# Four plain tiles instead of six, a pass of the output projection of their own, and a last pass that adds to a sum put into PSUM

## The chip, the cores and the metric

The kernel runs on one core of a Trainium2 chip. The metric is the device time of one execution in microseconds; lower is better. The inputs are already in the chip's memory when the time begins.

## The reference, cut to what matters

Two request groups (512 prompt tokens and 32 sample tokens, 544 in all) go through two layers of a streaming encoder. Each layer is feed-forward, mixer, feed-forward, so there are four feed-forward blocks; they take most of the time, and the change is in them alone.

```python
def swiglu(x, w_gate, w_up, w_down):
    a = jnp.einsum('btd,df->btf', x, w_gate)      # d = 1024, f = 2816
    b = jnp.einsum('btd,df->btf', x, w_up)
    return jnp.einsum('btf,fd->btd', jax.nn.silu(a) * b, w_down)
# in each layer, with gains g of the norms:
x = x + 0.5 * rms_norm(swiglu(rms_norm(x, g[0]), ...), g[1])
x = x + rms_norm(mixer(rms_norm(x, g[2])), g[3])
x = x + 0.5 * rms_norm(swiglu(rms_norm(x, g[4]), ...), g[5])
```

## The kernel before

**Numbers in two parts.** All matrix products are float32-accurate, made of three passes of the engine's rounded float32: each factor is split into a high part (ScalarE, a copy that rounds) and a low part (VectorE, the factor minus its high part), and `mm3` issues high x high, high x low and low x high. So each product of a 128x128 weight tile with 272 tokens is three matmuls, and the tokens come in two halves, H = 0 and 1. One weight set is loaded by SyncE's queue into `w_raw` (four slots of 128x1024, two groups of two units in flight), split into `w_hi` and `w_lo`, and used by TensorE. A slot's next load waits until its low part is made; its next high part waits until TensorE has left it.

**A feed-forward block** has 22 hidden tiles of 128 and runs in this order on TensorE:

1. The plain part: hidden tiles 0 to 5, one after the other. `in_half` makes gate and up of one tile for one half: 2 x 8 x 3 = 48 matmuls, so 96 a tile and 576 in all. VectorE takes each result out of PSUM times the norm's factor, ScalarE applies silu, and the two split the hidden tile.
2. The other 16 hidden tiles are eight pairs. For a pair, gate (step q even) and up (q odd) are 2x2 block products made with seven block products instead of eight: `seven`, 7 x 4 x 3 = 84 matmuls a step. Its left factors (parts of x and their sums, `part_of`) are made during the plain part; its right factors are sums of weight blocks (`sums`, three instructions on VectorE), split in four pieces (`split_seven`).
3. The output projection ("down") comes in two parts, because not all hidden tiles fit at once. Part 0 covers hidden tiles 0 to 9 (six plain, two pairs) and stands behind the first four steps of `seven`; part 1 covers tiles 10 to 21 behind the other twelve. A part is 16 units (m, H): output tile m of 8, half H. `down_unit` runs a unit in two pieces, u = 0 for the first eight hidden tiles and u = 1 for the rest; the first four units run all their u = 0 pieces ahead of their u = 1 pieces. Part 0's results are copied from PSUM to `y` by ScalarE (`down_half`); part 1's are added to `y` by VectorE (`add_half`), and ScalarE then squares and scales them (`down_result`).

The loops that call these on PE, ACT and DVE are written out by hand, and so is each engine's order; nothing is reordered later. GpSimd sums the squares. At a block's end (`boundary`, `update` on the engines) VectorE adds the normed result to x half by half, and the next sub-layer's first `in_half` waits tile by tile for `xlo`.

**Lines.** `mm3` is L777 to L779. L631 and L634 are the high and the low part of a plain or output weight, L676 and L679 those of a product step, L657 to L661 the sums, L1684 and L2042 the split of the left factors, L1989 the read of a gate, L2005 the low part of a plain hidden tile, L2068 that of a pair, L1625 `down_half`, L1635 the square, L1921 `add_half`, L1976 `xlo`.

## Time and profile before

| | |
|---|---|
| time, median of 3 runs | 1950.31 us (1947.32 to 1950.62) |
| the profiled execution | 1950.23 us; its span 1948.3 us |
| TensorE busy | 1927.8 us, 15984 matmuls |
| VectorE busy | 1274.9 us |
| ScalarE busy | 1012.5 us |
| GpSimd busy | 204.5 us |
| granted TensorE clock | 0.997 of full |

The span runs from the first to the last instruction of the execution; the time holds 1.9 us around it. A busy time is the sum over an engine's instructions. Matmuls overlap, each of them is recorded with some 0.29 us, so how fast they follow one another is read from windows (time over count) and not from the duration of one.

### The profile page before, as it was taken

The numbers are of one execution on the slowest core, as the hardware profiler recorded it, in microseconds if no ns is written. First come the engines' busy times: TensorE is split into PE (matmuls) and PEld (weight loads), VectorE is DVE, ScalarE is ACT, GpSimd is POOL, SyncE is SP. The second block draws the span as 40 slices with busy tenths as digits, with TensorE's granted clock in tenths as the row PEclk, the third lists the DMA queues.
The fourth block names the chain that finished last, engine by engine and source line by source line (L and its number), as shares of the span: only waits on it lengthen the run. The fifth ranks groups of instructions, "written<-read, shape, count | busy, mean of one in ns | idle before, by whom it ended". The sixth has DMA issues, their size and how long they took to land.

```text
span 1948.3 us, 38106 instructions
## 1 busy us (share of the span) xinstructions
PE 1927.8 (99%) x15984; PEld 1875.3 (96%) x15984; DVE 1274.9 (65%) x1652; ACT 1012.5 (52%) x1925; POOL 204.5 (10%) x221
## 2 busy tenths in 40 slices
PE   9999999999999999999999999999999999999997
PEld 9999999999669999999999999999997999999997
DVE  7853884674673886378559844784667488448845
ACT  7443664531584655366546543664438555436642
POOL 0000000200362100000020000001236200000012
PEclk9999999999999999999999999999999999999999
DMA  5232323332311222233323123222341221232232
GB/s 181 73 95 93 109 87 98 98 104 77 122 45 44 78 75 88 87 109 108 94 82 108 66 82 112 90 103 86 107 123 47 75 93 66 82 114 87 103 91 70
DMA packets 59018, 177.90 MB, mean 91 GB/s; under 512 B 7057, under 2 KB 15585, under 8 KB 58721
## 3 DMA queue, kind: packets, MB, share of 16 engines
q1 hardware_dynamic: 56720, 167.66, 26.5%
q0 software_dynamic: 2128, 7.80, 1.3%
q8 instruction: 128, 2.10, 0.5%
q14 instruction: 42, 0.34, 0.1%
HBM read 168.26 MB, written 5.36 MB: 89 GB/s over the span
## 4 chain that ended last, share of the span: by engine, by line
PE 93%; DVE 5%; issue 1%; ACT 1%; DMA 0%; DVEq 0%; SPq 0%; ACTq 0%
PE psum L779 29%; PE psum L777 29%; PE psum L778 28%; PE psum L1091 1%; PE psum L1077 1%; PE psum L1210 1%; DVE y L1894 1%; DVE xlo L1976 1%; PE psum L999 1%; DVE rstd L1883 1%; DVE w_lo L634 1%; PE psum L1054 1%; PE psum L1193 1%; PE psum L1165 1%; DVE x L1901 1%
## 5 line engine op out<-in xcount | busy, mean ns | idle before, releaser
L777 PE MATMUL psum<-xhi,w_hi 128*128 128x272 f32 x1824 | 529.8, 290 | 1.7 <-DVE xlo L1976 1.3
L779 PE MATMUL psum<-xhi,w_lo 128*128 128x272 f32 x1824 | 525.7, 288 | 0.0
L778 PE MATMUL psum<-xlo,w_hi 128*128 128x272 f32 x1824 | 524.9, 288 | 0.0
L779 PE MATMUL psum<-h_hi,w_lo 128*128 128x272 f32 x1216 | 351.6, 289 | 0.0
L777 PE MATMUL psum<-h_hi,w_hi 128*128 128x272 f32 x1216 | 349.8, 288 | 0.0
L778 PE MATMUL psum<-h_lo,w_hi 128*128 128x272 f32 x1216 | 349.6, 287 | 0.0
L777 PEld LDWEIGHTS psum<-xhi,w_hi 128*128 128x128 f32 x1824 | 343.5, 188 | 5.7 <-DVE xlo L1976 2.3
L634 DVE TENSOR_TENSOR w_lo<-w_raw,w_hi 128x1024 fp32r<-128x1024 f32 (+1 forms) x198 | 204.2, 1058 | 214.6 <-ACT w_hi L631 214.5
L778 PEld LDWEIGHTS psum<-xlo,w_hi 128*128 128x128 f32 x1824 | 343.4, 188 | 0.4
L779 PEld LDWEIGHTS psum<-xhi,w_lo 128*128 128x128 f32 x1824 | 342.8, 188 | 0.0
L631 ACT ACTIVATE w_hi<-w_raw 128x1024 fp32r<-128x1024 f32 (+1 forms) x198 | 170.2, 882 | 203.9 <-PE psum L779 203.8
L679 DVE TENSOR_TENSOR w_lo<-w_raw,w_hi 128x1024 fp32r<-128x1024 f32 x128 | 156.5, 1223 | 117.5 <-ACT w_hi L676 116.1
L778 PEld LDWEIGHTS psum<-h_lo,w_hi 128*128 128x128 f32 x1216 | 229.0, 188 | 0.0
L777 PEld LDWEIGHTS psum<-h_hi,w_hi 128*128 128x128 f32 x1216 | 228.8, 188 | 0.0
L779 PEld LDWEIGHTS psum<-h_hi,w_lo 128*128 128x128 f32 x1216 | 228.5, 188 | 0.0
L777 PE MATMUL psum<-corner,w_hi 128*128 128x272 f32 x768 | 221.8, 289 | 2.1 <-DVE w_lo L679 2.1
L778 PE MATMUL psum<-corner,w_hi 128*128 128x272 f32 x768 | 222.1, 289 | 0.0
L779 PE MATMUL psum<-corner,w_lo 128*128 128x272 f32 x768 | 222.1, 289 | 0.0
L676 ACT ACTIVATE w_hi<-w_raw 128x1024 fp32r<-128x1024 f32 x128 | 135.1, 1055 | 37.3 <-PE psum L779 37.3
L779 PE MATMUL psum<-xlo,w_lo 128*128 128x272 f32 x512 | 148.2, 290 | 0.0
L777 PEld LDWEIGHTS psum<-corner,w_hi 128*128 128x128 f32 x768 | 144.8, 189 | 3.1 <-DVE w_lo L679 2.9
L778 PE MATMUL psum<-xhi,w_hi 128*128 128x272 f32 x512 | 147.4, 288 | 0.0
(301 smaller groups left out, 3556.3 us busy)
## 6 DMA issues: line engine op xcount, KB each, us to landing
w_raw<-in_w_gate_up SPq DMA_DIRECT2D x172, 512.0 KB, 4.1
w_raw<-in_w_down SPq DMA_DIRECT2D x64, 512.0 KB, 3.6
w_raw<-in_w_down SPq DMA_DIRECT2D x32, 256.0 KB, 3.7
w_raw<-in_even_in SPq DMA_DIRECT2D x16, 512.0 KB, 3.9
w_raw<-in_odd_in SPq DMA_DIRECT2D x10, 512.0 KB, 4.3
w_raw<-in_w_down SPq DMA_DIRECT2D x32, 128.0 KB, 3.6
w_raw<-in_even_out SPq DMA_DIRECT2D x8, 512.0 KB, 3.8
w_raw<-in_odd_out SPq DMA_DIRECT2D x8, 512.0 KB, 4.3
```

The lines of the kernel that those rows point to most:

```text
L631: nc.scalar.activation(hi[:, cols], raw, ACT.Copy).then_inc(w_hi_done, 1)
L634: nc.vector.tensor_tensor(lo[:, cols], raw, hi[:, cols].bitcast(F32), ALU.subtract).then_inc(w_lo_done, 1)
L676: nc.scalar.activation(hi, raw, ACT.Copy).then_inc(w_hi_done, 1)
L679: nc.vector.tensor_tensor(lo, raw, hi.bitcast(F32), ALU.subtract).then_inc(w_lo_done, 1)
L777: nc.tensor.matmul(out, s_hi, m_hi, start=first, stop=False, skip_group_check=skip)
L778: nc.tensor.matmul(out, s_hi, m_lo, start=False, stop=False, skip_group_check=skip)
L779: return nc.tensor.matmul(out, s_lo, m_hi, start=False, stop=last, skip_group_check=skip)
L999: return nc.tensor.matmul(psum[rows, b, cols], q, k, start=False, stop=True, skip_group_check=True)
L1054: nc.tensor.matmul(psum[rows, bank + e, c:c + w], qN[r, p, q:q + 64], kN[r, p, 0:w], start=i < 2, stop=True, skip_group_check=True)
L1077: mm = nc.tensor.transpose(psum[0:kw, 4 + e, j * P:(j + 1) * P], pr[:, e, col:col + kw], ident[:])
L1091: return nc.tensor.matmul(psum[64 * e:64 * e + 64, bank, cols], v, probs, start=first, stop=True, skip_group_check=True)
L1165: mm = nc.tensor.matmul(psum[64 * half:64 * half + 64, bank + d, cols], qtC[r, tile, q0:q0 + HD], kdup[r, tile // 4, keys], start=True, st ...
```

## The change

The plain part shrinks to four hidden tiles, and nine pairs take the other 18 (18 steps, six of them ahead of part 0). The plain tiles get a pass of the output projection of their own, `first_pass`, right behind them: 16 units over four hidden tiles each, whose weights are four new groups ("first", 512 columns a unit). ScalarE copies its results into tiles 4 to 7 of `h_gate` and `h_raw` (`hold`). Part 0 then covers the six hidden tiles of the first three pairs (four in u = 0, two in u = 1); VectorE adds its results to the held ones and writes `y` (`add_held`). Part 1 covers twelve hidden tiles as before, but its PSUM banks are filled first with `y` by ScalarE (`put`), its matmuls add to what is there (no `start`), and ScalarE squares and scales straight out of PSUM; `add_half` is gone. `unit_tiles`, the loads and the waits for freed slots follow the new sizes.

```diff
-PLAIN = 6
-KDOWN = (10, 12)
+PLAIN = 4
+KDOWN = (6, 12)
+UNIT = (4, 8)
+HIDDEN = ((0, 1, 2, 3, 8, 9), tuple(range(12)))
+HELD = 4
 PAIRS = [(f, f + 1) for f in range(PLAIN, KF, 2)]
 SEVEN = 2 * len(PAIRS)
-SEVEN_A = KDOWN[0] - PLAIN
+SEVEN_A = KDOWN[0]
...
-KINDS = {"ffn": [("in", f) for f in range(PLAIN)] + [("seven", q) for q in range(SEVEN_A)] +
+KINDS = {"ffn": [("in", f) for f in range(PLAIN)] + [("first", i) for i in range(4)] + [("seven", q) for q in range(SEVEN_A)] +
...
         def pair_tiles(p):
-            f = PAIRS[p][0]
-            t = f if f < KDOWN[0] else f - KDOWN[0]
+            t = HIDDEN[0][2 * p] if 2 * p < KDOWN[0] else HIDDEN[1][2 * p - KDOWN[0]]
             return slice(t, t + 2)
+        def held(m, H):
+            return (h_gate if m < KD // 2 else h_raw)[:, HELD + m % 4, HALF[H]]
...
-                    pe.wait_ge(y_added, 2 * KD * (ffn_no(s) - 1) + 14)
+                    pe.wait_ge(y_scaled, 2 * KD * (ffn_no(s) - 1) + 14)
...
-                        pe.wait_ge(proj_read, P0[s] + 2 * PLAIN - 4 + (2 if name == "T1" else 1) + q)
+                        pe.wait_ge(first_read, 2 * KD * n + 9 + banks[name])
...
-                    hidden = KDOWN[0] * part + (KDOWN[part] if u else KD)
-                    pe.wait_ge(hlo_ready, 2 * PLAIN * (n + 1))
-                    pe.wait_ge(pair_lo, len(PAIRS) * n + (hidden - PLAIN) // 2)
+                    hidden = KDOWN[0] * part + (KDOWN[part] if u else UNIT[part])
+                    pe.wait_ge(pair_lo, len(PAIRS) * n + hidden // 2)
                 bank = DOWN_BANKS[part][down_order(part).index((m, H)) % 4]
-                for k in range(KD, last + 1) if u else range(KD):
-                    w = slice((k - KD * u) * P, (k - KD * u + 1) * P)
-                    mm = mm3(psum[:, bank, 0:TH], hi[:, w], lo[:, w], h_hi[:, k, HALF[H]], h_lo[:, k, HALF[H]],
-                             k == 0, k == last)
+                for k in range(UNIT[part], last + 1) if u else range(UNIT[part]):
+                    w, t = slice((k - UNIT[part] * u) * P, (k - UNIT[part] * u + 1) * P), HIDDEN[part][k]
+                    mm = mm3(psum[:, bank, 0:TH], hi[:, w], lo[:, w], h_hi[:, t, HALF[H]], h_lo[:, t, HALF[H]],
+                             k == 0 and part == 0, k == last, part > 0)
...
+            def first_pass(s):
+                n = ffn_no(s)
+                def some(i, tiles):
+                    m, H, bank = i // 2, i % 2, i % 8
+                    g, u = G0[s] + PLAIN + m // 2, m % 2
+                    pe.wait_ge(w_lo_done, splits_at(g) + u + 1)
+                    for k in tiles:
+                        w = slice(k * P, (k + 1) * P)
+                        mm = mm3(psum[:, bank, 0:TH], w_hi[:, slot(g, u), w], w_lo[:, slot(g, u), w],
+                                 h_hi[:, k, HALF[H]], h_lo[:, k, HALF[H]], k == 0, k == PLAIN - 1)
+                    return mm
+                pe.wait_ge(hlo_ready, 2 * (PLAIN * (n + 1) - 1))
+                for i in range(6):
+                    if i in (0, 4):
+                        pe.wait_ge(proj_read, P0[s] + 2 * PLAIN - (0 if i else 2))
+                    some(i, range(PLAIN - 1))
+                pe.wait_ge(hlo_ready, 2 * PLAIN * (n + 1))
+                for i in range(6):
+                    some(i, (PLAIN - 1,)).then_inc(first_done, 1)
+                for i in range(6, 2 * KD):
+                    if i >= 8:
+                        pe.wait_ge(first_read, 2 * KD * n + i - 7)
+                    some(i, range(PLAIN)).then_inc(first_done, 1)
             def down(s, part):
...
+                                pe.wait_ge(first_read, 2 * KD * (n + 1))
...
                         elif u == 0:
-                            if i == 0:
-                                pe.wait_ge(corner_added, 2 * (SEVEN * (n + 1) - 1))
-                                pe.wait_ge(corner_copied, 2 * (SEVEN * (n + 1) - 1))
-                            elif i == 3:
-                                pe.wait_ge(corner_added, 2 * SEVEN * (n + 1))
-                                pe.wait_ge(corner_copied, 2 * SEVEN * (n + 1))
+                            pe.wait_ge(y_put, 2 * KD * n + i + 1)
...
-                    pe.wait_ge(y_added if part else y_half, 2 * KD * n + i - 3)
+                    pe.wait_ge(*((y_put, 2 * KD * n + i + 1) if part else (y_half, 2 * KD * n + i - 3)))
...
+            def hold(s, i):
+                act.wait_ge(first_done, 2 * KD * ffn_no(s) + i + 1)
+                nc.scalar.activation(held(i // 2, i % 2), psum[:, i % 8, 0:TH], ACT.Copy).then_inc(first_read, 1)
             def down_result(s, i):
                 order = down_order(1)
                 m, H = order[i]
-                act.wait_ge(y_added, 2 * KD * ffn_no(s) + i + 1)
+                whole = psum[:, DOWN_BANKS[1][i % 4], 0:TH]
+                act.wait_ge(y_ready, y_event(s, m, H) + 1)
                 if i >= 4:
                     act.wait_ge(ysq_summed, total_event(s, *order[i - 4]) + 1)
-                nc.scalar.activation(scratch[:, i % 4, :], y[:, m, HALF[H]], ACT.Square).then_inc(ysq_ready, 1)
-                nc.scalar.activation(y[:, m, HALF[H]], y[:, m, HALF[H]], ACT.Copy,
+                nc.scalar.activation(scratch[:, i % 4, :], whole, ACT.Square).then_inc(ysq_ready, 1)
+                nc.scalar.activation(y[:, m, HALF[H]], whole, ACT.Copy,
                                      scale=post_gains[:, s, m:m + 1]).then_inc(y_scaled, 1)
+                if 4 <= i + 3 < 2 * KD:
+                    put(s, i + 3)
+            def put(s, i):
+                n, (m, H) = ffn_no(s), down_order(1)[i]
+                if i == 0:
+                    act.wait_ge(y_half, 2 * KD * (n + 1))
+                    act.wait_ge(corner_added, 2 * (SEVEN * (n + 1) - 1))
+                elif i == 3:
+                    act.wait_ge(corner_added, 2 * SEVEN * (n + 1))
+                elif i >= 4:
+                    act.wait_ge(y_scaled, 2 * KD * n + i - 3)
+                nc.scalar.activation(psum[:, DOWN_BANKS[1][i % 4], 0:TH], y[:, m, HALF[H]], ACT.Copy).then_inc(y_put, 1)
...
                         part_high(s, 3)
+                for i in range(2 * KD):
+                    hold(s, i)
+                    if i == 1:
+                        split_unit(act, "act", g + PLAIN + 2, 0)
+                    elif i == 3:
+                        split_unit(act, "act", g + PLAIN + 2, 1)
                         part_high(s, 4)
+                    elif i == 5:
+                        split_unit(act, "act", g + PLAIN + 3, 0)
+                    elif i == 7:
+                        split_unit(act, "act", g + PLAIN + 3, 1)
+                        part_high(s, 5)
+                        part_high(s, 6)
+                    elif i in (9, 11, 13, 15):
+                        split_seven(act, "act", s, 0, (i - 9) // 2)
+                keep(s, 0, "B11")
...
+                                for i in range(3):
+                                    put(s, i)
                             split_unit(act, "act", down_group(s, part, 0), 1)
...
-                        for i in range(2 * KD):
-                            down_half(s, i)
-                            if i == 1:
-                                split_unit(act, "act", down_group(s, 0, 2), 1)
-                            elif i in (2, 5, 6, 9, 10):
-                                split_group(act, "act", down_group(s, 0, {2: 3, 5: 4, 6: 5, 9: 6, 10: 7}[i]))
-                            elif i in (13, 14):
-                                split_seven(act, "act", s, SEVEN_A, i - 13)
+                        split_unit(act, "act", down_group(s, 0, 2), 1)
+                        for m in range(3, KD):
+                            split_group(act, "act", down_group(s, 0, m))
+                        split_seven(act, "act", s, SEVEN_A, 0)
...
                     load_table(ACT.Sqrt)
+                    put(s, 3)
...
+            def add_held(s, i):
+                n, (m, H) = ffn_no(s), down_order(0)[i]
                 if i == 0:
-                    dve.wait_ge(y_half, 2 * KD * (n + 1))
-                dve.wait_ge(y_ready, y_event(s, m, H) + 1)
-                half = y[:, m, HALF[H]]
-                nc.vector.tensor_tensor(half, half, psum[:, DOWN_BANKS[1][i % 4], 0:TH], ALU.add).then_inc(y_added, 1)
+                    dve.wait_ge(first_read, 2 * KD * (n + 1))
+                dve.wait_ge(y_ready, y_event(s, m, H, 0) + 1)
+                nc.vector.tensor_tensor(y[:, m, HALF[H]], held(m, H), psum[:, DOWN_BANKS[0][i % 4], 0:TH],
+                                        ALU.add).then_inc(y_half, 1)
...
+                        split_unit(dve, "dve", down_group(s, 0, 2), 0)
+                        for i in range(2 * KD):
+                            add_held(s, i)
+                            if i == 2:
+                                split_unit(dve, "dve", down_group(s, 0, 2), 1)
+                            elif i in (3, 6, 7, 10, 11):
+                                split_group(dve, "dve", down_group(s, 0, {3: 3, 6: 4, 7: 5, 10: 6, 11: 7}[i]))
+                            elif i == 13:
+                                sums(dve, s, SEVEN_A)
+                            elif i == 14:
+                                split_seven(dve, "dve", s, SEVEN_A, 0)
+                                split_seven(dve, "dve", s, SEVEN_A, 1)
                         continue
                     split_unit(dve, "dve", down_group(s, 1, 2), 0)
...
-                        add_half(s, i)
```

Three places on two engines, as the built programs have them; numbers in brackets are the semaphores that an instruction waits for.

The first is ScalarE behind the split of the third left factor (`part_high`, `corner_56`). Before, the last two plain tiles follow (L1601 silu, L1606 high part of h), mixed with the splits for the first product step (L676):

```order
L1601 ACTIVATE gate_even<-gate_even 128x544 [waits gate_scaled]
L1606 ACTIVATE h_hi<-gate_even 128x544 [waits h_ready]
L676 ACTIVATE w_hi<-w_raw 128x1024 [waits proj_ready,raw_in0]
L676 ACTIVATE w_hi<-w_sum 128x1024 [waits proj_ready,w_summed]
L1684 ACTIVATE xhi<-sum_63 128x4x272 [waits proj_ready,part_ready]
L1684 ACTIVATE xlo<-sum_66 128x4x272 [waits proj_ready,part_ready]
L676 ACTIVATE w_hi<-w_raw 128x1024 [waits proj_ready,w_summed]
L1601 ACTIVATE scratch<-scratch 128x544 [waits gate_scaled]
```

After, the 16 copies of `hold` (L1663) stand there, with the splits of the first pass's last two groups (L645) and of the product step (L690) between them:

```order
L1737 ACTIVATE xhi<-sum_63 128x4x272 [waits proj_ready,part_ready]
L1663 ACTIVATE h_gate<-psum 128x272 [waits first_done] x2
L645 ACTIVATE w_hi<-w_raw 128x512 [waits first_done,raw_in0]
L1663 ACTIVATE h_gate<-psum 128x272 [waits first_done] x2
L645 ACTIVATE w_hi<-w_raw 128x512 [waits first_done,raw_in1]
L1737 ACTIVATE xlo<-sum_66 128x4x272 [waits proj_ready,part_ready]
L1663 ACTIVATE h_gate<-psum 128x272 [waits first_done] x2
```

The silu and high-part steps of two plain tiles went, sixteen reads of PSUM came, and the product step's splits moved behind the ninth of them.

The second is VectorE where output part 0 ends and the next product step's weights are made. Before, the low parts of output tile 7 (L634), the sums (L657 to L661) and the product step's low parts (L679) follow one another without a wait for a result:

```order
L634 TENSOR_TENSOR w_lo<-w_raw,w_hi 128x1024 [waits w_hi_done]
L634 TENSOR_TENSOR w_lo<-w_raw,w_hi 128x256 [waits w_hi_done]
L657 TENSOR_TENSOR w_sum<-w_raw 128x1024 [waits w_lo_done,raw_in1,raw_in0]
L659 TENSOR_TENSOR w_raw<-w_raw,w_sum 128x512 [waits w_summed]
L661 TENSOR_TENSOR w_sum<-w_raw 128x512 [waits w_summed]
L679 TENSOR_TENSOR w_lo<-w_raw,w_hi 128x1024 [waits w_hi_done]
L679 TENSOR_TENSOR w_lo<-w_sum,w_hi 128x1024 [waits w_hi_done]
```

After (`add_held` is L1976, the low parts L648 and L693, the sums L671 to L675):

```order
L648 TENSOR_TENSOR w_lo<-w_raw,w_hi 128x512 [waits w_hi_done]
L648 TENSOR_TENSOR w_lo<-w_raw,w_hi 128x256 [waits w_hi_done]
L1976 TENSOR_TENSOR y<-h_raw,psum 128x272 [waits y_ready] x2
L671 TENSOR_TENSOR w_sum<-w_raw 128x1024 [waits w_lo_done,raw_in1,raw_in0]
L673 TENSOR_TENSOR w_raw<-w_raw,w_sum 128x512 [waits w_summed]
L675 TENSOR_TENSOR w_sum<-w_raw 128x512 [waits w_summed]
L1976 TENSOR_TENSOR y<-h_raw,psum 128x272 [waits y_ready]
L693 TENSOR_TENSOR w_lo<-w_raw,w_hi 128x1024 [waits w_hi_done]
L693 TENSOR_TENSOR w_lo<-w_sum,w_hi 128x1024 [waits w_hi_done]
L1976 TENSOR_TENSOR y<-h_raw,psum 128x272 [waits y_ready]
```

The adds of units 12 to 15 (four, the first two in one row), which wait for TensorE, now stand between them.

The third is VectorE at the boundary behind part 1 of the first block. Before, `add_half` (L1921) stands between the steps of `update` (L1894 and L1901) and of `xlo` (L1976):

```order
L1894 TENSOR_TENSOR y<-y,rstd 128x2x272
L1901 TENSOR_TENSOR x<-x,y 128x2x272 [waits dve_step]
L1976 SCALAR_TENSOR_TENSOR xlo<-x,gains,xhi 128x272 [waits xhi_ready] x2
L1921 TENSOR_TENSOR y<-y,psum 128x272 [waits y_ready]
L634 TENSOR_TENSOR w_lo<-w_raw,w_hi 128x1024 [waits w_hi_done] x2
L1901 TENSOR_TENSOR x<-x,y 128x2x272 [waits dve_step]
```

After, the same steps (L1952, L1959, L2030) with no add between them:

```order
L1952 TENSOR_TENSOR y<-y,rstd 128x2x272
L1959 TENSOR_TENSOR x<-x,y 128x2x272 [waits dve_step]
L2030 SCALAR_TENSOR_TENSOR xlo<-x,gains,xhi 128x272 [waits xhi_ready] x2
L648 TENSOR_TENSOR w_lo<-w_raw,w_hi 128x1024 [waits w_hi_done] x2
L1959 TENSOR_TENSOR x<-x,y 128x2x272 [waits dve_step]
```

The add went; two more went from the same stretch, one between two earlier steps of `update` and one behind the `xlo` rows that follow, and one from ahead of it.

## Rows read from the trace of the kernel before

**Rows 1.** The page: engines' busy time, and the clock granted to TensorE in 40 slices.

```profile
PE 1927.8 (99%) x15984; PEld 1875.3 (96%) x15984; DVE 1274.9 (65%) x1652; ACT 1012.5 (52%) x1925; POOL 204.5 (10%) x221
...
PEclk9999999999999999999999999999999999999999
```

**Rows 2.** The page: the chain that ended last, by engine.

```profile
PE 93%; DVE 5%; issue 1%; ACT 1%; DMA 0%; DVEq 0%; SPq 0%; ACTq 0%
```

**Rows 3.** Windows, TensorE alone: busy (instructions), clock, DMA share, GB/s.

```profile
124.00:184.20 60.20, 60.20 (x481) 1.00 0.31 100
184.20:310.80 126.60, 126.60 (x1009) 1.00 0.28 97
310.80:383.50 72.70, 72.70 (x581) 1.00 0.32 96
```

**Rows 4.** Whom TensorE waited for: us in total, times, longest us.

```profile
PE psum L777 <- DVE w_lo L679: 2.1, 4, 0.5
...
PE psum L777 <- DVE xlo L1976: 1.3, 4, 0.6
```

**Rows 5.** Timeline of TensorE where the second product step begins: start, us.

```profile
91.21 0.29 PE L779 MATMUL psum<-xlo,w_lo 128*128 128x272 f32 x1
92.01 0.39 PE L777 MATMUL psum<-corner,w_hi 128*128 128x272 f32 x1 [0.52 <-DVE w_lo L679]
```

**Rows 6.** The same at the boundary behind the first feed-forward block.

```profile
386.14 0.29 PE L779 MATMUL psum<-xhi,w_lo 128*128 128x272 f32 x1
386.54 0.39 PE L777 MATMUL psum<-xhi,w_hi 128*128 128x272 f32 x1
...
398.82 0.28 PE L779 MATMUL psum<-xhi,w_lo 128*128 128x272 f32 x1
399.28 0.39 PE L777 MATMUL psum<-xhi,w_hi 128*128 128x272 f32 x1 [0.18 <-DVE xlo L1976]
```

**Rows 7.** Timeline of VectorE at that boundary.

```profile
380.25 0.42 DVE L1921 TENSOR_TENSOR y<-y,psum 128x272 f32<-128x272 f32 x1
```

**Rows 8.** Timeline of the end of the kernel, VectorE and ScalarE.

```profile
1936.18 0.44 DVE L1921 TENSOR_TENSOR y<-y,psum 128x272 f32<-128x272 f32 x1 [3.44 <-PE psum L779]
1936.65 0.43 ACT L1635 ACTIVATE scratch<-y 128x272 f32<-128x272 f32 x1 [3.67 <-DVE y L1921]
```

**Rows 9.** Timeline of VectorE behind plain tile 3, and at the first product steps.

```profile
56.82 0.72 DVE L1989 TENSOR_TENSOR scratch<-psum,rstd 128x544 f32<-128x544 f32 x1 [2.00 <-PE psum L779]
...
60.99 0.72 DVE L2005 TENSOR_TENSOR h_lo<-scratch,h_hi 128x544 fp32r<-128x544 f32 x1
...
88.16 1.22 DVE L657 TENSOR_TENSOR w_sum<-w_raw 128x1024 f32<-128x1024 f32 x1
...
90.74 1.22 DVE L679 TENSOR_TENSOR w_lo<-w_raw,w_hi 128x1024 fp32r<-128x1024 f32 x1
```

**Rows 10.** Timeline of VectorE behind the first product stage.

```profile
128.18 1.29 DVE L2068 TENSOR_TENSOR h_lo<-h_raw,h_hi 128x1088 fp32r<-128x1088 f32 x1 [0.85 <-ACT h_hi L1676]
```

**Rows 11.** VectorE ahead of the second product stage, and the loads it needs (SPq).

```profile
172.35 1.23 DVE L657 TENSOR_TENSOR w_sum<-w_raw 128x1024 f32<-128x1024 f32 x1 [1.19 <-DMA w_raw<-in_w_gate_up]
...
167.10 4.56 SPq L706 DMA_DIRECT2D w_raw<-in_w_gate_up  x4
```

**Rows 12.** Groups on VectorE by shape: busy, mean ns | idle before.

```profile
L679 DVE TENSOR_TENSOR w_lo<-w_sum,w_hi 128x512 fp32r<-128x512 f32 x64 | 43.8, 684 | 0.0
...
L1921 DVE TENSOR_TENSOR y<-y,psum 128x272 f32<-128x272 f32 x64 | 27.9, 436 | 119.7 <-PE psum L779 119.3
```

**Rows 13.** Groups on ScalarE by shape.

```profile
L631 ACT ACTIVATE w_hi<-w_raw 128x1024 fp32r<-128x1024 f32 x135 | 140.3, 1054 | 177.2 <-PE psum L779 177.2
...
L676 ACT ACTIVATE w_hi<-w_sum 128x512 fp32r<-128x512 f32 x64 | 40.5, 632 | 23.6 <-PE psum L779 23.6
...
L1625 ACT ACTIVATE y<-psum 128x272 f32<-128x272 f32 x64 | 25.0, 390 | 92.3 <-PE psum L779 92.3
...
L1684 ACT ACTIVATE xhi<-sum 128x1088 fp32r<-128x1088 f32 x8 | 8.8, 1105 | 0.0
```

104 lines of the change are left out of this document (39 added, 65 removed).

## The prediction

> **What bounds the kernel now.** First the page's busy times and clock row, then the chain that ended last, then windows of TensorE alone. The first shows TensorE busy for 1927.8 of 1948.3 us at full clock, VectorE for two thirds and ScalarE for half [rows 1]; the second puts 93% of the chain on TensorE [rows 2]. So time goes only where matmuls are removed or where TensorE stands still. The windows give its pace: output part 0 (480 matmuls and one neighbour) takes 60.20 us, the last twelve product steps (1008) 126.60 us, output part 1 with its neighbours 72.70 us [rows 3]: 60.20/480 = 0.1254 and 126.60/1008 = 0.1256 us a matmul, the same in the product steps and in the projection. No window holds a hole. So 0.1256 us is what one matmul is worth.
>
> Then the holes. The table of waits names two kinds, four times each [rows 4]. One is where the second product step of a block begins: starts 0.80 us apart where the pace is 0.13, so 0.67 us lost, waiting for the low part of a weight [rows 5]; all four blocks have it. VectorE began the sums for that step at 88.16 and ended the first low part at 90.74 + 1.22 = 91.96 [rows 9]; it was late because the last plain tiles, the left factors' low parts and the first step's weights had all been queued ahead. The other is behind a block: starts 0.40 and 0.46 us apart, so 0.27 + 0.33 = 0.60 us lost [rows 6]; three blocks have a feed-forward or mixer stage behind them. Last, behind the final unit, VectorE's add (0.44 us) and then ScalarE's square stand on the chain with nothing beside them [rows 8].
>
> **The change, part by part.** *Matmuls.* Two plain tiles cost 2 x 96 = 192, the pair that replaces them two steps of 84 = 168. The projection stays at 22 x 8 x 2 x 3 = 1056 a block, in three passes. So 24 fewer a block, 96 in all: 96 x 0.1256 = **-12.1 us**. TensorE's load of weights is in the pace already.
>
> The Trainium skill's page "TensorE: Matmul & The Clock Gate", section "Back-to-back issue gap", gives a gap of columns/2.4 + 2.5 ns at full clock, for 272 columns 116 ns, and says that pairs of weight load and matmul are paced by both. By its formula the term would be 11.1 us; the row's 125.6 ns decides.
>
> *The new pass at its start.* E is the end of the last plain `in_half`. The six first units take hidden tiles 0 to 2 (54 matmuls, 6.8 us) before tile 3 is wanted. Behind plain tile 3 today, VectorE starts at 56.82 and its low part ends at 61.71, 4.9 us later [rows 9]; it will be shorter by half of two splits. Slack 1.9 us. The four plain tiles no longer have a fifth behind them, and this is what hides them instead.
>
> *Its second weight pair.* Unit 8 starts at E + 96 x 0.1256 = 12.1 us and wants the low part of group 2, which VectorE makes behind the tile's low part (4.9), two sums of left factors and three low parts of them (five of 1.29) and then 0.68 [rows 9, 10, 12]: 12.0 us by full durations. But consecutive instructions start some 0.08 us sooner than that, and the two splits ahead take 0.68 and not 1.22. So about 11 us, no wait; from the other side, 0.3 us a block.
>
> *VectorE up to the product steps.* By the same durations, everything between E and the last piece of the first step is 25.1 us: 4.9 - 1.1 for tile 3, nine instructions of 1.29 for the left factors (the row of their shape), 4 x 0.68 for splits, the sums 2.58 (88.16 to 90.74), 3 x 1.22 + 0.68 for the pieces [rows 9, 10, 12]; besides it waits for the splits' high parts (ScalarE's last comes behind its copy of unit 15, near E + 25). TensorE wants the first piece at E + 24.1 and the last 9 us after. The first is ready three pieces earlier, near 22. No wait; and the sums of the second step now start at E + 26 for a step at E + 34.7, where before they ran late. So the first kind of hole closes: 4 x 0.67 = **-2.7 us**.
>
> *ScalarE in the pass.* 16 copies of 0.39, four splits of 0.63, three left factors of 1.11, 3 x 1.05 + 0.63 for the step's pieces [rows 13]: 15.9 of 24.1 us. PSUM has eight banks, so a unit may come seven later than its copy. Free.
>
> *Six steps and not four ahead of part 0.* The same steps as the twelve of the window, which have no hole. Free beyond their matmuls.
>
> *Part 0.* Its first pieces now cover only 4 x 12 x 0.1256 = 6.0 us and not 12.1, and then the last pair is wanted. Today its low part ends at 128.18 + 1.29 = 129.47, 5.5 us behind the part's start at 124.0 [rows 3, 10]. ScalarE and VectorE each split 512 and not 1024 columns ahead of it, so nearer 4.7. Slack 0.6 to 1.3 us. A unit now lasts 18 x 0.1256 = 2.26 us and not 3.77. Its u = 0 weights go into a slot that TensorE leaves 0.75 us ahead of the end of a unit and are wanted 2.26 us behind that end: 3.0 us for a high part (0.63), the add that waits for the unit's end (0.44) and the low part (0.68) [rows 12, 13], 0.75 + 0.44 + 0.68 = 1.9 us. Slack 1.1 us. The adds are on VectorE, which idled there.
>
> *Part 0 to the next product step.* With S the start of that step, unit 13 ends at S - 4.5. VectorE adds (0.44), sums (2.58), adds (0.44) and makes the first low part (1.22) [rows 9, 12], which comes to S + 0.2 by full durations and S by overlapped ones, plus some 0.1 for the signals. Today all this lies far ahead: the sums began at 172.35, 11.9 us before 184.20 [rows 3, 11]. The loads take 172.35 - 167.10 = 5.3 us [rows 11]; issued behind tile 6's low part, which follows the add of unit 10 (end S - 11.3, + 0.44 + 0.68 = S - 10.2), they land at S - 4.9, before the sums want them. So 0 to 0.5 us a block, I take 0.2: **+0.8 us**.
>
> *Puts.* ScalarE writes three banks inside the last product step (3 x 0.39) and the fourth behind the last pair; TensorE wants that one 9 us into part 1. The trace has no copy from `y` to PSUM; the nearest row is the copy the other way, 0.39 [rows 13], and a block's sixteen would be 6.2 us of ScalarE's idle half. Each later put comes two units (9 us) ahead of its unit. Free; if not free at the part's start, 0.4 a block.
>
> *Boundary.* Three adds of 0.43 [rows 7] leave VectorE's queue ahead of the `xlo` that TensorE waits for, two before the first hole and all three before the second; ScalarE's square comes an add earlier. Both holes (0.27, 0.33) are shorter than that. ScalarE's put there fills an idle stretch. 3 x 0.60 = **-1.8 us**. At the very end the add goes: 1936.65 - 1936.18 = **-0.5 us** [rows 8].
>
> *Loads.* The same bytes in more pieces; queued behind the same kind of wait. Nothing.
>
> Sum: -12.1 - 2.7 + 0.8 - 1.8 - 0.5 = -16.3 us. Against the profiled execution's 1950.23 us that is 1933.9; the median of the runs, 1950.31, is 0.1 above it. **I predict 1934 us.** 0.2% (4 us) is what a measurement of this kernel tells from no change.
>
> **Rivals.** *(1) The holes stay or move, only the matmuls go.* VectorE gets 16 adds into its densest stretches, and three slacks above are about a microsecond. If the closed holes come back as others of their size and part 0's end costs its upper bound, 0.5: 1950.2 - 12.1 + 2 = 1940; with the second weight pair and the puts at their bounds too, (0.3 + 0.4) x 4 = 2.8, 1943. For it: the slacks; against it: each is positive by rows. 1937 to 1943.
>
> *(2) PSUM is emptied too slowly.* Three passes are read out instead of two, 16 reads more and 16 writes more a block, all by ScalarE. It decides when ScalarE's work in the first pass passes 24.1 us; it is 15.9, so each of those copies would have to take 0.9 and not 0.39 us. Then TensorE waits 0.5 us or more a unit, and at 0.5 us on 16 units in four blocks, +32 us, 1966. The Trainium skill, page "Trainium Kernel Development and Optimization", section "Best Practices", says to mind PSUM pressure, as a denser TensorE does not speed up its evacuation; the rows have ScalarE half idle.
>
> *(3) Slower by part 0's short units.* If high part, add and low part for a unit's weights take longer than 3.0 us, each of twelve units waits. The gain is used up at 16.3/48 = 0.34 us each, so when the 1.9 us become 3.35; at 0.5 us, +24 - 16 = +8, 1958. It would need a load that lands late or an add that waits a full unit. No row shows either.
>
> *(4) Nothing moves,* because another engine already paces TensorE: 1950. Against it, a pace equal to 0.2% in two stages with different partners.
>
> **How the numbers follow.** My forecast (1930.5 to 1937): 0.66. Rival 1: 0.22. Rivals 2 and 3: 0.04 each. Rival 4: 0.02; what I have not thought of: 0.02, either side. The range takes the forecast and most of rival 1: 1930 to 1941. Faster by over 0.2% (below 1946.4): 0.90; within: 0.04; slower: 0.06.
>
> **What would show it.** TensorE with 96 matmuls fewer in its count; windows of product steps and of part 0 still at 0.1256 us a matmul; no wait for a low part at a block's second product step; starts at the boundaries 0.13 us apart; a new small wait for a low part where part 0 ends; the square on the chain right behind the last matmul. The prediction is wrong if part 0's window is longer than 288 x 0.1256 = 36.2 us, if the first pass is longer than 24.1 us, or if the pace itself changes where ScalarE writes PSUM beside TensorE.

## The result, and the profile after

The changed kernel takes **1930.88 us**, the median of four executions (1930.58 to 1932.5), beside 1949.74 us (1947.32 to 1950.62) for the kernel before on the same chip: ratio 0.9898, 95% interval 0.9876 to 0.992. That is 18.9 us; 16.3 were forecast. The profiled execution took 1932.5 us with a span of 1930.4, beside 1950.23 and 1948.3. When the comparison was repeated, the medians lay 14.7 us (e2) and 15.1 us (e10) apart. So the first question is which of these is the change.

The page's busy times, clock row and chain (as [rows 1, 2]):

```profile
PE 1912.4 (99%) x15888; PEld 1861.9 (96%) x15888; DVE 1299.6 (67%) x1716; ACT 1060.2 (55%) x2077; POOL 196.3 (10%) x221
...
PEclk9999999999999999999999999999999999999999
...
PE 94%; DVE 4%; issue 1%; ACT 1%; DMA 0%; POOL 0%; DVEq 0%; ACTq 0%; SPq 0%
```

96 matmuls are gone and TensorE is still the chain. Windows of TensorE in the first block (as [rows 3]): first pass, six product steps, part 0, the step into the next product stage, its twelve steps, part 1:

```profile
56.55:80.63 24.08, 24.08 (x195) 1.00 0.33 110
80.63:143.99 63.36, 63.36 (x507) 1.00 0.26 84
143.99:180.15 36.16, 36.16 (x290) 1.00 0.36 117
180.15:180.40 0.25, 0.16 (x3) 1.00 0.00 0
180.40:307.23 126.83, 126.83 (x1009) 1.00 0.29 97
307.23:379.81 72.58, 72.58 (x580) 1.00 0.31 98
```

The first three are 192, 504 and 288 matmuls (the windows count a neighbour or two more) at 0.1254, 0.1257 and 0.1256 us: no hole in them, and the pace is that of before. New is the quarter microsecond at 180.15. TensorE there and at the same place of the second block, and whom it waited for in the whole kernel (as [rows 4, 5]; of its nine waits, this one is where the change is):

```profile
180.02 0.29 PE L796 MATMUL psum<-h_hi,w_lo 128*128 128x272 f32 x1
180.40 0.39 PE L794 MATMUL psum<-corner,w_hi 128*128 128x272 f32 x1
180.63 0.28 PE L795 MATMUL psum<-corner,w_hi 128*128 128x272 f32 x1
...
813.76 0.29 PE L796 MATMUL psum<-h_hi,w_lo 128*128 128x272 f32 x1
815.25 0.40 PE L794 MATMUL psum<-corner,w_hi 128*128 128x272 f32 x1 [1.20 <-DVE w_lo L693]
```

```profile
PE psum L794 <- DVE w_lo L693: 1.2, 1, 1.2
```

Starts are 0.38 us apart in blocks 1, 3 and 4 and 1.49 in block 2. VectorE and the loads (SPq) at the two places (as [rows 11]):

```profile
176.19 1.22 DVE L671 TENSOR_TENSOR w_sum<-w_raw 128x1024 f32<-128x1024 f32 x1
...
179.12 1.22 DVE L693 TENSOR_TENSOR w_lo<-w_raw,w_hi 128x1024 fp32r<-128x1024 f32 x1
```

```profile
803.85 4.04 SPq L720 DMA_DIRECT2D w_raw<-in_w_gate_up  x4
...
811.03 1.23 DVE L671 TENSOR_TENSOR w_sum<-w_raw 128x1024 f32<-128x1024 f32 x1 [1.02 <-DMA w_raw<-in_w_gate_up]
```

In block 1 the sums start right behind the add of unit 13, and the first low part ends at 180.34, TensorE's start. In block 2 the loads landed 7.1 us after the first of them was issued, where the prediction counted 5.3 from issue to sums, so the sums waited 1.0 us more.

A boundary behind a block (as the second pair of [rows 6]) and the end (as [rows 8]):

```profile
394.41 0.29 PE L796 MATMUL psum<-xhi,w_lo 128*128 128x272 f32 x1
394.75 0.40 PE L794 MATMUL psum<-xhi,w_hi 128*128 128x272 f32 x1
```

```profile
1918.52 0.29 PE L796 MATMUL psum<-h_hi,w_far_lo 128*128 128x272 f32 x1
...
1918.85 0.40 ACT L1674 ACTIVATE scratch<-psum 128x272 f32<-128x272 f32 x1 [3.73 <-PE psum L796]
```

The first hole of the boundary is gone and the second shrank from 0.46 to 0.34 between starts here (in other executions it is gone too, and a gap of 0.37 stands at the total's matmul instead). At the end the square starts as soon as the matmul's result is there.

**What the medians hid.** The even mixer's attention isn't touched by the change. Windows of TensorE there, before and then after; the third figure is the granted clock:

```profile
512.00:518.00 6.00, 4.56 (x49) 0.73 0.00 0
518.00:524.00 6.00, 6.00 (x46) 0.70 0.00 0
524.00:530.00 6.00, 6.00 (x104) 1.00 0.01 3
```

```profile
506.00:512.00 6.00, 4.57 (x61) 1.00 0.00 0
512.00:518.00 6.00, 6.00 (x48) 0.72 0.00 0
518.00:524.00 6.00, 6.00 (x104) 1.00 0.01 3
```

Before, (0.27 + 0.30) x 6 / 0.5 = 6.8 us were spent at the lower level (1.2 GHz), after 0.28 x 6 / 0.5 = 3.4. Each time the fall comes at a wait of TensorE for `probsE`, 1.4 us. Before, TensorE waited from 513.5 to 514.9 and the clock fell at 514.7; after, it waited from 508.9 to 510.4 and the clock fell at 512.1. At half the clock that costs half the stretch: 3.4 us in the profile of before, 1.7 in that of after. It was my base of 1950.23 us that held those 3.4 us.

### The profile page after: what moved, and what is told of

It is laid out like the page before. It is cut to its first block, busy times and chain, and to the rows that moved or that the text cites. A ratio compares the mean times of both kernels' runs of the same rounds, so it can differ in the third digit from the quotient of the medians.

```text
span 1930.4 us, 38306 instructions
## 1 busy us (share of the span) xinstructions
PE 1912.4 (99%) x15888; PEld 1861.9 (96%) x15888; DVE 1299.6 (67%) x1716; ACT 1060.2 (55%) x2077; POOL 196.3 (10%) x221
## 4 chain that ended last, share of the span: by engine, by line
PE 94%; DVE 4%; issue 1%; ACT 1%; DMA 0%; POOL 0%; DVEq 0%; ACTq 0%; SPq 0%
PE psum L796 29%; PE psum L794 29%; PE psum L795 29%; PE psum L1129 1%; PE psum L1115 1%; PE psum L1248 1%; DVE y L1952 1%; PE psum L1037 1%; PE psum L1231 1%; DVE rstd L1941 1%; PE psum L1092 1%; PE psum L1203 1%; DVE xlo L2030 0%; DVE w_lo L648 0%; PE psum L1081 0%
## 5 line engine op out<-in xcount | busy, mean ns | idle before, releaser
L794 PE MATMUL psum<-xhi,w_hi 128*128 128x272 f32 x1632 | 473.9, 290 | 0.2
L796 PE MATMUL psum<-xhi,w_lo 128*128 128x272 f32 x1632 | 470.4, 288 | 0.0
L795 PE MATMUL psum<-xlo,w_hi 128*128 128x272 f32 x1632 | 469.6, 288 | 0.0
L794 PEld LDWEIGHTS psum<-xhi,w_hi 128*128 128x128 f32 x1632 | 307.4, 188 | 3.5 <-issue 2.0
L795 PEld LDWEIGHTS psum<-xlo,w_hi 128*128 128x128 f32 x1632 | 307.2, 188 | 0.5
L796 PEld LDWEIGHTS psum<-xhi,w_lo 128*128 128x128 f32 x1632 | 306.7, 188 | 0.0
L648 DVE TENSOR_TENSOR w_lo<-w_raw,w_hi 128x1024 fp32r<-128x1024 f32 (+1 forms) x214 | 184.3, 886 | 163.5 <-ACT w_hi L645 163.0
L645 ACT ACTIVATE w_hi<-w_raw 128x1024 fp32r<-128x1024 f32 (+1 forms) x214 | 160.9, 770 | 216.0 <-PE psum L796 214.0
L693 DVE TENSOR_TENSOR w_lo<-w_raw,w_hi 128x1024 fp32r<-128x1024 f32 x144 | 176.1, 1223 | 114.4 <-ACT w_hi L690 112.7
L794 PE MATMUL psum<-corner,w_hi 128*128 128x272 f32 x864 | 249.1, 288 | 1.5 <-DVE w_lo L693 1.2
L795 PE MATMUL psum<-corner,w_hi 128*128 128x272 f32 x864 | 249.9, 289 | 0.0
L796 PE MATMUL psum<-corner,w_lo 128*128 128x272 f32 x864 | 249.8, 289 | 0.0
L690 ACT ACTIVATE w_hi<-w_raw 128x1024 fp32r<-128x1024 f32 x144 | 152.1, 1057 | 37.2 <-PE psum L796 37.1
L795 PE MATMUL psum<-xhi,w_hi 128*128 128x272 f32 x576 | 165.8, 288 | 0.0
L794 PE MATMUL psum<-xlo,w_hi 128*128 128x272 f32 x576 | 165.4, 287 | 0.0
```

Source lines behind the costliest of these rows:

```text
L645: nc.scalar.activation(hi[:, cols], raw, ACT.Copy).then_inc(w_hi_done, 1)
L648: nc.vector.tensor_tensor(lo[:, cols], raw, hi[:, cols].bitcast(F32), ALU.subtract).then_inc(w_lo_done, 1)
L690: nc.scalar.activation(hi, raw, ACT.Copy).then_inc(w_hi_done, 1)
L693: nc.vector.tensor_tensor(lo, raw, hi.bitcast(F32), ALU.subtract).then_inc(w_lo_done, 1)
L794: nc.tensor.matmul(out, s_hi, m_hi, start=first, stop=False, skip_group_check=skip)
L795: nc.tensor.matmul(out, s_hi, m_lo, start=False, stop=False, skip_group_check=skip)
```

## The experiments

All are compared with the kernel before on the same chip. "Level" is the lowest cluster of a kernel's times, those of a mean granted clock of 0.998 or more.

**e1, the kernel before once more.** No edit. 

> The kernel before, unchanged, against itself. The profiled execution of before has a stretch at half clock of 6.83 us in the even mixer, that of after one of 3.41 us. Theory A (my sum was right, the rest is this stretch): executions of one and the same program differ by the length of that stretch, so times fall on levels about 1.7 us apart (half of 3.41), between 1947 and 1951, and the longer ones show the lower mean clock; ratio 1.000. Theory B (the stretch belongs to the kernel's order of work): all its times lie within 1 us of each other, near 1950, and its profile shows 6.8 us at half clock again.

1949.0 us (1947.26 to 1950.84, 12 executions), ratio 0.9998 (0.9987 to 1.0008). Its times stand in three clusters: four at 1947.3 to 1947.9 (clock 0.998), three at 1948.7 to 1949.1, five at 1950.1 to 1950.8 (0.997, 0.996). The profiled one (1947.88) has no stretch at the lower clock in the attention. The clusters are 0, 1.6 and 3.3 us above the level, about what stretches of 0, 3.4 and 6.8 us cost (0, 1.7 and 3.4).

**e2 and e10, the changed kernel twice more.** No edit. 

> The changed kernel, unchanged, once more and in five rounds. Theory A: times on levels 1.7 us apart between 1929 and 1933, and the ratio to before nearer 0.9916 (-16.3 us) than 0.9898 when both sides are drawn from the same mixture; -16 to -18 us. Theory B: -18.5 to -20 us again, 1930.5 us with a stretch at half clock of at most 3.4 us each time, and its gain over my sum is the change's own.

> The changed kernel unchanged, again. My theory for the spread of one kernel's times: TensorE runs for 0, 3.41 or 6.83 us (or longer) at half the clock in the even mixer's attention, and each such stretch costs half its length. So its times fall on a ladder: about 1930.7 where there is none, 1932.4 and 1934.1 with one or two units of 3.41 us, and higher up to 1941 where the mean clock is 0.993 or 0.994. Profile: span minus half of the stretch is 1928.6 within 0.4 us. Rival (the spread is from loads at the start or from another engine): profiles with equal stretches differ by more than 1 us.

e2: 1934.15 us (1932.98 to 1940.45), ratio 0.9929 (0.9911 to 0.9947). e10: 1934.02 (1931.95 to 1934.21), ratio 0.9913 (0.9892 to 0.9934). The profiled spans are 1931.9 with 6.8 us at the lower clock and 1932.1 with twice 3.4 us; less half of that 1928.5 and 1928.7, and the first one 1930.4 - 1.7 = 1928.7. Equal within 0.2, as the ladder says. The second 3.4 us of e10 lie at another place, from 587.5, behind the attention's last matmuls of 32 columns and 2.9 us after a wait of 0.46 us; e3 below has one there too:

```profile
584.00:590.00 6.00, 5.54 (x70) 0.79 0.01 3
```

The single times don't fall on clean rungs. The executions with a mean clock of 0.998 stand at 1930.6 to 1931.1 us in the first comparison, at 1931.95 in e10 and at 1933.0 and 1933.3 in e2, and what the last two spent 2 us more on isn't shown: they weren't profiled. The mean clock alone can't tell, for it reads 0.997 with 3.4 us of lower clock (after) and with 6.8 (before, e10).

**e4, twenty-four matmuls put back in each block.** Two units of the first pass are computed twice:

```diff
+                    if i >= 2 * KD - 2:
+                        some(i, range(PLAIN))
                     some(i, range(PLAIN)).then_inc(first_done, 1)
```

> The changed kernel in which the last two units of the first pass are computed twice, 24 matmuls more a block, 96 in all; the second time replaces the first, the output is the same. My theory: 96 x 0.1256 = 12.1 us more than the changed kernel, every hole as before. Rival (part of what the change gave is not matmuls but slack elsewhere): 9 us or less, since the added time lets loads, VectorE and ScalarE catch up and the remaining holes (2 us) close.

1944.84 us (1941.61 to 1945.5), ratio 0.9973, 10.7 above e2. Its first pass:

```profile
56.43:83.53 27.10, 27.10 (x219) 1.00 0.29 98
```

27.10 - 24.08 = 3.02 us for 24 matmuls, 0.126 each, 12.1 in four blocks; the gap in block 2 shrank meanwhile by 1.1 us, as its load landed sooner, which leaves 11.0. The term stands. (By the gap formula of the Trainium skill's page "TensorE: Matmul & The Clock Gate", section "Back-to-back issue gap", which the page gives for isolated matmuls, 24 of them would be 2.8 us, an estimate; the measured 3.02 decides.)

**e5 and e6, the put by itself.** e5 is the kernel before with only the last pass changed (put, adding in PSUM, no `add_half`); e6 is the changed kernel with `add_half` back:

```diff
-                whole = psum[:, DOWN_BANKS[1][i % 4], 0:TH]
-                act.wait_ge(y_ready, y_event(s, m, H) + 1)
+                act.wait_ge(y_added, 2 * KD * ffn_no(s) + i + 1)
...
-                nc.scalar.activation(psum[:, DOWN_BANKS[1][i % 4], 0:TH], y[:, m, HALF[H]], ACT.Copy).then_inc(y_put, 1)
```

> The kernel before (six plain tiles, eight pairs, two passes) with the last pass changed alone: ScalarE puts y into PSUM, the matmuls add to it, add_half is gone. By the prediction's terms it gains the boundary (3 x 0.60) and the end (0.5), -2.3 us; by what the changed kernel's trace shows at its boundaries (0.8 to 1.0 each) -2.9 to -3.5 us; so about 1945.5 to 1946.5 where before has 1948.8. The four 0.80 gaps at the second product step stay, matmuls 15984. Rival (writing PSUM from ScalarE slows TensorE): pace above 0.1256 us in part 1, and no gain. Rival (the new put waits): gaps at the start of part 1, up to 0.4 us a block, gain about 1 us.

> The changed kernel with add_half back in the last pass (no put, no adding in PSUM). It loses what e5 gains: 2.3 us over the changed kernel by the prediction's terms, 2.9 to 3.5 by the boundaries seen; so 1933.5 to 1937.5. Matmuls 15888, product-step holes still closed, the gaps of 0.37 and 1.49 behind part 0 unchanged, the boundary's two gaps of about 0.4 back. Rival (the two parts of the change need each other, because VectorE has no room for 12 + 16 adds): new waits in the product steps or in part 1, and a time nearer before.

e5: 1945.66 us (1943.75 to 1948.52, 11 executions) beside 1948.67, ratio 0.9982 (0.9973 to 0.999): -3.0, and at the level 1943.75 beside 1947.03, -3.3. ScalarE's put by shape in e5, not in any trace before:

```profile
L1647 ACT ACTIVATE psum<-y 128x272 f32<-128x272 f32 x64 | 25.1, 402 | 0.0
```

402 ns where 390 was the nearest row. The part-1 window of the changed kernel, with puts, is 578 matmuls in 72.58 us, that of before, without them, 579 in 72.70 [rows 3]: 0.1256 us each in both, so ScalarE's writing of other banks costs TensorE nothing here. e6: 1935.01 us (1934.47 to 1941.71). Its boundary has the gap again:

```profile
383.06 0.29 PE L796 MATMUL psum<-xhi,w_lo 128*128 128x272 f32 x1
383.46 0.39 PE L794 MATMUL psum<-xhi,w_hi 128*128 128x272 f32 x1
383.70 0.29 PE L795 MATMUL psum<-xlo,w_hi 128*128 128x272 f32 x1
```

Its profile has no lower-clock stretch and a block-2 gap of 1.88; against e14 below (0.37) that is 1.5 of the 4.6 us of span between them, and the rest is the put. So the put is worth 3.0 to 3.3 us and my 2.3 were short. The rival of a needed pair (no room for 28 adds) is out.

**e3, the sums one add earlier.** VectorE makes the sums behind the add of unit 12 and the first low part behind that of unit 13:

```diff
-                            elif i == 13:
+                            elif i == 12:
                                 sums(dve, s, SEVEN_A)
-                            elif i == 14:
+                            elif i == 13:
                                 split_seven(dve, "dve", s, SEVEN_A, 0)
+                            elif i == 14:
```

> The changed kernel with VectorE's sums for the second product stage one add earlier, and the first low part behind the add of unit 13 instead of unit 14. My theory: the wait of 0.25 us (1.36 us in one block, where the load landed late) at the start of that stage comes from VectorE's queue of adds and sums, so it goes: 1 to 2.1 us less than the changed kernel in the profile, starts 0.13 us apart there. Rival: it is the load that lands too late in all blocks; then the sums only wait longer and the holes stay: 0 us.

1931.84 us (1929.7 to 1938.63), ratio 0.9913 (0.9895 to 0.993), 2.3 below e2, though its profile spent 10.2 us at the lower clock. The gaps in blocks 1, 3 and 4 are gone. In block 2 1.11 stays, and its row names the load:

```profile
813.41 1.23 DVE L671 TENSOR_TENSOR w_sum<-w_raw 128x1024 f32<-128x1024 f32 x1 [2.92 <-DMA w_raw<-in_w_gate_up]
```

So VectorE's order sets three of the gaps and the load the fourth.

**e7, part 0's adds twice.**

```diff
+                if i > 0:
+                    dve.wait_ge(y_half, 2 * KD * n + i)
+                nc.vector.tensor_tensor(scratch[:, 2, :], held(m, H), psum[:, DOWN_BANKS[0][i % 4], 0:TH], ALU.add)
```

> The changed kernel with every add_held done twice on VectorE (once into scratch, not read). Tests the slack of part 0's short units and the shortage at its end. My sum gives 1.1 us of slack in a unit, so part 0's window stays 36.2 us; behind part 0 the sums and the first low part are queued behind two more adds (units 12 to 14 each have a double), so each of the four gaps there grows by 0.4 to 1.2 us: +1.6 to +5 us in all. Rival 3 (part 0's units already at their limit): each of twelve units a block waits about 0.4 us, +19 us. Rival (the gap behind part 0 is set by the loads, not by VectorE's adds): only block 2's gap matters and it does not grow by the full amount.

1934.23 us (1933.37 to 1941.55), ratio 0.9933 (0.9916 to 0.9951). Part 0 and the step behind it:

```profile
144.08:180.43 36.35, 36.35 (x290) 1.00 0.36 116
```

```profile
180.30 0.29 PE L796 MATMUL psum<-h_hi,w_lo 128*128 128x272 f32 x1
181.36 0.39 PE L794 MATMUL psum<-corner,w_hi 128*128 128x272 f32 x1 [0.78 <-DVE w_lo L693]
```

Sixteen more adds a block cost part 0 0.19 us; the gap behind it is 1.07 in all four blocks, 0.69 more than where the load comes in time. The short units have their slack and rival 3 is refuted; the place behind part 0 has none.

**e8, the first pass's copies twice** on ScalarE, the extra one into scratch:

```diff
+                nc.scalar.activation(scratch[:, 2, :], psum[:, i % 8, 0:TH], ACT.Copy)
```

> The changed kernel with every hold (copy out of PSUM in the first pass) done twice on ScalarE, 16 x 0.39 = 6.2 us more of ScalarE a block in a pass of 24.1 us of which my sum has 15.9 busy. By my sum it costs nothing in units; at most the high parts of the first product step come later, 0 to 1 us a block, so 0 to +4 us. Rival 2 (PSUM emptied too slowly): TensorE waits in each unit, 0.4 us x 16 x 4 = +25 us.

1932.15 us (1930.91 to 1940.9), ratio 0.9929 (0.9907 to 0.995): no slower than the changed kernel. All engines in its first pass, TensorE, its weight loads, VectorE, ScalarE, GpSimd:

```profile
56.55:80.63 24.08, 24.08 (x195) 24.08 (x194) 22.17 (x24) 20.69 (x44) 0.00 (x0) 1.00 0.36 110
```

ScalarE busy for 20.7 of 24.1 us (17.6 in the changed kernel, where my sum had 15.9) and TensorE without a hole: rival 2 is refuted. The Trainium skill ("Trainium Kernel Development and Optimization", "Best Practices") advises to mind PSUM pressure; no run here shows any, as eight banks took this much without a hole.

**e9, the load sooner.** e3, and the low part of output tile 6 ahead of the add of unit 10:

```diff
-                            elif i in (3, 6, 7, 10, 11):
-                                split_group(dve, "dve", down_group(s, 0, {3: 3, 6: 4, 7: 5, 10: 6, 11: 7}[i]))
+                            elif i in (3, 6, 7, 9, 11):
+                                split_group(dve, "dve", down_group(s, 0, {3: 3, 6: 4, 7: 5, 9: 6, 11: 7}[i]))
```

> e3 (sums and first split behind part 0 one add earlier on VectorE) and besides the low part of output tile 6 ahead of the add of unit 10 instead of behind it, so that the loads for the next product step are issued some 0.4 us sooner. If the gap that e3 left in the second block (1.11 us between starts) is set by the landing of these loads, it shrinks by 0.3 to 0.5 us and the other three stay closed; time with an undisturbed clock 0.3 to 0.5 us below e3's 1929.7. Rival (VectorE's queue sets it): the gap stays 1.1 us or a wait for the high part comes ahead of the add, no gain.

1930.39 us (1929.12 to 1932.42), ratio 0.99 (0.9875 to 0.9925). The gap in block 2 is 0.76 where e3 had 1.11, and the load was under way for 6.7 us in both. That is the 0.3 to 0.5 expected, but the load alone moves this gap by more (0.37 to 1.88 in profiles with the changed kernel's order there), so one profile of each doesn't prove it.

**e11, e13 and e14, ten matmuls in the attention's wait.** The same edit in the changed kernel (e11, e14) and in the kernel before (e13); e12 is e9 with it:

```diff
+                    if n == 3:
+                        pe.wait_ge(v_copied, 7)
+                        for _ in range(10):
+                            nc.tensor.matmul(psum[:, 4, 0:TH], xhi[:, 0, 0:P], xhi[:, 0, HALF[0]], start=True, stop=True)
                     if n < 2:
                         pe.wait_ge(vb_copied, 2 * n + 2)
```

> The changed kernel with ten added matmuls of 272 columns (their result is not used, some 1.2 us of TensorE) in the 1.4 us in which TensorE waits for probsE ahead of the fourth group of attention scores, the wait after which the profile shows the clock falling. If that wait brings the fall, no execution has a half-clock stretch near 510 us, the ladder closes to its lowest rung, 1930.7 to 1931.5, and the median lies there. Rival (the fall comes from the low activity of the whole stretch, or from outside the kernel): stretches of 3.41 or 6.83 us are still seen and the times are spread as without the added matmuls.

> The kernel before with the ten added matmuls (272 columns, result not used) in the 1.4 us wait for probsE in the even mixer's attention. If the wait brings the fall of the clock, its times close up at the lowest level of before, 1946 to 1947.5 us with a spread under 1 us, where before itself spreads from 1947.0 to 1956.6; and e13 minus e14 is the change alone: 16.3 us by my sum, 16.6 by the executions without a stretch. Rival (before's stretch has another cause, or the gain over the sum is real): times still spread over 3 us, or a difference from e14 of 18 us or more.

> The changed kernel with the same ten matmuls, as e11, on the same chip as e13: 1929.4 to 1931 us with a spread under 1 us. The gap behind part 0 in the second block is between 0.37 and 1.5 us between starts, by how late its load lands in this execution.

> e9 and the ten added matmuls together, the candidate for the fastest version: if both theories hold 1929.3 us with little spread, ratio to before near 0.991; if only e9's does, a spread from 1929.3 up to 1939.

| | us, median | from | to | executions |
|---|---|---|---|---|
| e13, before with it | 1947.38 | 1946.99 | 1948.03 | 11 |
| e14, changed with it | 1930.26 | 1929.87 | 1930.38 | 4 |
| e11, the same | 1929.75 | 1929.43 | 1929.95 | 4 |
| e12, e9 with it | 1928.6 | 1928.49 | 1928.78 | 4 |

All 23 executions have a mean clock of 0.998 or 0.999; of the 71 of the kernel before beside the experiments (e1's own included) 30 had. TensorE in e11, as a timeline and in windows:

```profile
508.65 1.52 PE L1069 MATMUL psum<-xhi 128*128 128x272 f32 x10
510.16 0.88 PE L1096 MATMUL psum<-kN,qN 64*64 64x64 f32 x16
```

```profile
512.00:518.00 6.00, 6.00 (x86) 1.00 0.01 3
518.00:524.00 6.00, 6.00 (x88) 1.00 0.00 0
```

The added work fits into the wait, and the clock stays at full. e13 and e14 ran on one chip: 1947.38 - 1930.26 = **17.1 us** is the change with the clock at full throughout. But the pair differs in one thing more. In all four profiles of changed kernels that have the ten matmuls (e11, e12, e14, e15) the load of block 2 is in time, and in none of the three of the changed kernel as it is, where it costs 1.1 us. So as it is the change brings about 1 us less: 1947.32 against 1930.6 to 1931.1, the executions of the first comparison with a clock of 0.998, is 16.2 to 16.7 us.

What goes with the late load is in the traces. The DMA queues from the issue of the first to the landing of the second of the two loads that the sums wait for, in the first profile after (803.85 to 810.95) and then in e11 (802.08 to 806.76); packets, MB, share of the 16 engines:

```profile
q1 hardware_dynamic: 531, 1.98, 78.7%
q8 instruction: 1, 0.02, 1.6%
```

```profile
q1 hardware_dynamic: 359, 1.34, 79.7%
```

Queue 8, which the profile calls "instruction", moved one packet of 16 KB inside the first window and none inside the second, where the packet had started 1.8 us ahead of the issue. In seven profiles (after, e2, e3, e6, e8, e9, e10) such a packet starts 1.1 to 2.6 us behind the issue, and the two loads take 6.7 to 7.5 us. In the six others (e4, e7, e11, e12, e14, e15) it starts ahead of the issue or 4.5 us behind it, and they take 4.7 to 5.3. At other places it goes the same way, by less or as much: in block 1 a packet 1.1 us behind the issue comes with 5.4 to 5.9 us, and in block 3 of e12 one 3.1 us behind it with 6.6 and a gap of 0.57. No run moved that packet alone, so that it is the cause is not shown.

**e15, the ten matmuls behind that wait** (ahead of the scores but after the wait for `exp_done`). 

> The changed kernel with the ten matmuls behind the wait for probsE instead of ahead of it, so that TensorE's wait of 1.4 us stays. If the wait brings the fall of the clock, the times are spread as without them, 1931 to 1941, some of them at mean clocks of 0.997 and less, and 0.3 to 1.2 us later for the added work. Rival (any added work there keeps the clock): times as close together as e14's.

1931.45 us (1930.98 to 1934.65, five executions), four of them within 0.7 us at a clock of 0.998 and one at 0.996. The wait is still there:

```profile
510.62 1.53 PE L1072 MATMUL psum<-xhi 128*128 128x272 f32 x10 [1.43 <-ACT probsE L1449]
```

The forecast, times spread from 1931 to 1941, came for one of the five. One fall in five is fewer than before's 41 in 71 and more than none in 23, and five executions don't tell these apart. In the 13 profiles that keep the wait the clock fell there in seven: for 6.8 us where it fell 0.3 us before the wait's end to 0.1 behind it (before, e2, e3, e4), for 3.4 us where it fell 1.5 to 1.9 us behind (after, e5, e10). That filling the wait keeps the clock is shown; that the wait alone brings the fall, and not also how little TensorE does behind it, stays open.

## Why the prediction was off, by its own steps

The measured 1930.88 us lies at the lower edge of the range (1930 to 1941), 3.0 below the forecast 1933.9. The direction came as forecast and so did the terms' signs. The step that failed is the base; besides, three terms of the sum were mis-sized, and their errors nearly cancelled, which is luck.

**The base.** "Against the profiled execution's 1950.23 us that is 1933.9": the sum was taken from one execution's time and carried over to all executions of the changed kernel. That profile held 3.4 us that belong to a stretch of lower clock and not to the kernel; the page's clock row, 9 in each slice, didn't show it, and the 0.997 beside the span was the hint. In the first comparison three of the four changed executions had a mean clock of 0.998, and the median of before lay 2.4 us above its level of 1947.3: 18.9 - 2.4 = 16.5 us are left for the change. With 1947.3 in place of 1950.23 the same sum gives 1931.0, and 1930.88 was measured. In e2 and e10 the draw was the other way.

**The sizes.** The terms as forecast, and as the profiles of e13 and e14 (no such stretch in either, and block 2's load in time) show them:

| term | forecast | measured | from |
|---|---|---|---|
| 96 matmuls | -12.1 | -12.1 | e4's window |
| second product step's hole | -2.7 | -3.5 | 4 x 0.88 |
| part 0 to next step | +0.8 | +1.4 | 4 x 0.35; 1.1 more when block 2's load is late |
| boundaries | -1.8 | -2.6 | 3 x 0.88 |
| end | -0.5 | -0.5 | start gap 1.02 to 0.52 |
| sum | -16.3 | -17.3 | medians: -17.1 |

The spans of the two profiles differ by 17.6 us, of which 0.3 lies in the first 29 us, where the change does nothing. With the late load of the changed kernel as it is the sum is -16.2: the forecast -16.3 is met by -0.8 and -0.8 against +0.6 and +1.1.

The step that failed in the second and the fourth line is "0.80 us apart where the pace is 0.13, so 0.67 us lost". The matmul behind a wait also delays its own successor. Two more rows of before: the second one behind [rows 5], and the start of the first product step:

```profile
92.01 0.39 PE L777 MATMUL psum<-corner,w_hi 128*128 128x272 f32 x1 [0.52 <-DVE w_lo L679]
92.24 0.29 PE L778 MATMUL psum<-corner,w_hi 128*128 128x272 f32 x1
```

```profile
83.70 0.38 PE L777 MATMUL psum<-corner,w_hi 128*128 128x272 f32 x1
83.92 0.29 PE L778 MATMUL psum<-corner,w_hi 128*128 128x272 f32 x1
```

0.23 and 0.22 us where the pace is 0.13: 0.10 more per hole, and a small one at the first step's start that I hadn't counted and that also went. 0.67 + 0.10 + 0.10 = 0.88 within rounding. At a boundary 0.27 + 0.10 + 0.43 + 0.10 = 0.90 (the second hole is 0.46 in the first block of [rows 6] but 0.53 to 0.56 in the others and in e13), less 0.13 for a gap now at the total's matmul, and 0.1 more from small gaps between. (Of the four waits for `xlo` in [rows 4] only three are behind blocks; the longest, 0.6 us, is at 7.3 us, at the kernel's start.) The third line fails the same way (0.25 + 0.10), and by the late load.

**What held.** At full clock no matmul pace changed. The first pass took 24.08 us (24.1 forecast as its limit), part 0 36.16 (36.2). The second weight pair, the puts and part 0's last pair wait for nothing. "They land at S - 4.9" was right within 0.4 us at three places; in block 2 of the first profile the load took 7.1 us, and my bound of 0.5 us for that place had no room for it. The sign "starts at the boundaries 0.13 us apart" came for one of the two holes; 0.34 to 0.38 us stay at the other or at the total's matmul. Rivals 1 to 4 are out: the holes did not come back, except for part 0's end.

**What stays open.** Whether the packet of queue 8 is what makes that one load late: the gap in block 2 was 1.47 to 1.88 in four profiles of the changed kernel and its variants, 1.28 in e8 and 0.37 in four (e4, e11, e14, e15), in step with the packet's place, but no experiment varied it alone. And some executions lie 7 to 11 us above the level at a clock of 0.992 to 0.994: four of 75 of before, and eight of 51 of the changed kernel and its variants without the ten matmuls. None was profiled, so what they spend it on isn't shown, nor whether the change makes them more frequent.

The fastest version run is e12, 1928.6 us: 20.5 us below the 1949.09 of before beside it (ratio 0.9888, 0.9867 to 0.9908), 18.8 below e13, which has the clock at full too but ran on another chip, and 1.15 below e11.
